# Decoder step: GpSimd's subtractions behind the expert order, sums copied in halves, constant products where TensorE waits, two adaLN products at later attention units

## The chip, the cores and the metric

One core of one Trainium2 chip runs the whole program. The metric is the device time of one execution in microseconds (us); the median of three runs is quoted.

## The reference, cut to what matters

One inference step of a two-layer decoder for 320 tokens (256 of a prompt, 8 sequences of 8 new ones). Layer 0 mixes tokens by sliding-window attention, layer 1 by gated linear attention (GLA); each is followed by a mixture of 64 experts. All weights are fp32 and come from HBM.

```python
for layer in range(DEPTH):
    mod = (jax.nn.silu(c) @ ada_w[layer] + ada_b[layer])[:, None, :]      # adaLN: 12 blocks of 512 columns a layer
    sh1, sc1, g1, sh2, sc2, g2 = jnp.split(mod, 6, axis=-1)
    hmix = rms_norm(x, norm_mix_g[layer]) * (1.0 + sc1) + sh1
    out = attention or gla (hmix)
    x = x + g1 * out
    hffn = rms_norm(x, norm_ffn_g[layer]) * (1.0 + sc2) + sh2
    x = x + g2 * moe(hffn)            # sigmoid router, top 8 of 64 experts, plus one shared expert
return rms_norm(x, final_g), caches, states
```

## The kernel before, in words

Each engine has a program of its own, written out by hand and joined by semaphores; an engine takes its instructions in the order of the code. Weights stream through a ring of five 2 MB slots (`gu_ring`) and one of five 1 MB slots (`dn_ring`), issued in order by SyncE (SP).

- **Front.** The squares, their sum and the mean of x, then four adaLN blocks, one after the other: `ada_part(n)` (L480, eight products of 32 x 512 on TensorE), `ada_copy` (ScalarE, L486), `ada_fold` (L492, four products of 128 x 32), `ada_mod` (VectorE, L499). The next `ada_part` waits for the `ada_mod` before it. Behind them the q, k, v projections (L646) begin.
- **Attention.** A pipeline over 24 units: scores (L691), mask and maximum (VectorE L908, L915), exponential (ScalarE L831), normalisation (VectorE L923), turning of the probabilities (L713), copy (ScalarE L842), output (L727). In unit 2 VectorE also does `rope(2)` (L880 to L883). The table `AT_SLOT` says at which unit i the adaLN blocks 12 to 17 are multiplied; ScalarE copies such a block at the end of its own step i, TensorE folds it in step i + 1.
- **MoE, choice of experts.** TensorE turns h into token rows (L1544); ScalarE writes each twice, as fp32 (`tok32`) and rounded (`hi`); GpSimd subtracts them (`lo`, L1518). VectorE meanwhile picks the top 8 (L1626 to L1652), TensorE counts (L1570) and sorts, VectorE writes `order` (L1667), SP reads it and issues the experts' weights (L1453, L1457). Between these steps TensorE does the shared expert's up products (`shared_up`, L1559, four groups of 16).
- **MoE, passes.** 29 passes (`NP`) of two or four experts: up products (L1822), gathers for the next batch (L1763), turning (L1836), down products (L1853), and `combine` (L1785, L1788), which adds the pass before to the sums in PSUM. After the last pass comes `rest`, a branch that runs only if an expert got more tokens than it has slots; `any_left` loads the number that decides it into a register of each engine.
- **MoE, end.** ScalarE and VectorE copy the sums to SBUF (L1963 to L1970), TensorE turns them back (`back`, L1985), VectorE adds them to x (L402 to L407). After layer 0 come the next norm (L351, L357), two adaLN blocks and GLA (L1038 on); after layer 1 the rows are turned once more (L2046) for the final norm.

## Time and profile before

| what | value |
|---|---|
| runs | 1592.98, 1595.33, 1602.84 us; median 1595.33 |
| profiled execution: its own time, its span | 1602.87 us, 1600.8 us |
| granted TensorE clock, mean | 0.962 of full speed |
| TensorE busy | 1483.1 us (93% of the span) |
| VectorE, ScalarE, GpSimd busy | 413.9, 387.2, 49.3 us |
| DMA | 509.57 MB, mean 318 GB/s |

The span is from the first to the last instruction of the profiled execution; some 2 us lie around it. Busy shares are averages over stages with different limits: what one stage costs has to be read from its own stretch. Times in rows are us from the start of the span. A matmul of two fp32 operands stands as two records in the trace, so eight products are "x16".

### The profile page before, as it was taken

What the parts mean: (1) busy time and instruction counts of PE and PEld (TensorE: products, weight loads), DVE (VectorE), ACT (ScalarE), POOL (GpSimd) and SP (SyncE); (2) the same over time, 40 slices, a digit from 0 to 9 for tenths busy, and PEclk for the clock granted to TensorE, in tenths of its full rate; (3) what the DMA queues carried; (4) which work ended last, traced back from release to release, by engine and by line L of the source; (5) the groups of instructions that cost most, each with busy time, mean ns of one, the idle gap of its engine ahead of it and who ended that gap; (6) DMA issues with size and microseconds to landing.
All of it is one profiled execution on the core that took longest, in us unless ns stands there. A gap on an engine that the chain in (4) does not pass through costs nothing.

```text
span 1600.8 us, 20538 instructions
## 1 busy us (share of the span) xinstructions
PE 1483.1 (93%) x8192; PEld 757.5 (47%) x8192; DVE 413.9 (26%) x978; ACT 387.2 (24%) x1077; POOL 49.3 (3%) x86
## 2 busy tenths in 40 slices
PE   5997998899998899999899989989999999999895
PEld 2444665454453445444345445554444444544433
DVE  2116515121221212211253233432121112211113
ACT  2114404122221112121244212412222211212112
POOL 0000301000000000000100000100000000000000
PEclk9998899999999999999889998999999999999997
DMA  9977514899998999999942243188999999998971
GB/s 396 365 282 290 181 63 164 343 417 421 420 419 322 421 421 418 381 398 421 393 158 105 106 161 115 60 336 342 421 421 420 388 377 421 420 421 343 423 323 33
DMA packets 65888, 509.57 MB, mean 318 GB/s; under 512 B 7776, under 2 KB 8048, under 8 KB 10208
## 3 DMA queue, kind: packets, MB, share of 16 engines
q1 hardware_dynamic: 62064, 490.17, 74.9%
q0 software_dynamic: 3728, 18.07, 3.1%
q8 instruction: 67, 1.10, 0.3%
q14 instruction: 29, 0.24, 0.0%
HBM read 499.16 MB, written 11.01 MB: 319 GB/s over the span
## 4 chain that ended last, share of the span: by engine, by line
PE 80%; DMA 9%; ACT 3%; DVE 3%; issue 2%; SPq 1%; PEld 1%; PEldq 1%; ACTq 0%; DVEq 0%
PE bank L1822 24%; PE banks L1853 11%; DMA s_gu_ring<-in_moe_wu_dram 9%; PE banks L1763 7%; PE banks L426 5%; PE banks L1023 3%; PE ybank L1785 3%; PE banks L1785 3%; PE bank L1788 3%; PE banks L646 3%; PE bank L480 2%; PE banks L1051 2%; PE bank L492 1%; PE bank L1773 1%; PE banks L1028 1%
## 5 line engine op out<-in xcount | busy, mean ns | idle before, releaser
L1822 PE MATMUL bank<-s_gu_ring,s_hbuf 128*32 128x512 f32 (+1 forms) x2560 | 422.9, 613 | 31.6 <-DMA s_gu_ring<-in_moe_wu_dram 31.6
L1822 PEld LDWEIGHTS bank<-s_gu_ring,s_hbuf 128*32 128x32 f32 (+1 forms) x2560 | 134.9, 125 | 310.4 <-issue 310.4
L1853 PE MATMUL banks<-s_dn_ring,s_hTs 128*32 128x512 f32 (+1 forms) x1280 | 211.6, 597 | 2.4 <-ACT s_hTs L1899 2.4
L1951 DVE TENSOR_TENSOR s_ylo<-banks,s_yhi 128x512 fp32r<-128x512 f32 x116 | 80.3, 692 | 338.8 <-ACT s_yhi L1907 338.8
L1763 PE MATMUL banks<-s_sel,s_htok 128*128 128x512 f32 (+2 forms) x640 | 148.6, 381 | 0.5 <-issue 0.5
L1763 PEld LDWEIGHTS banks<-s_sel,s_htok 128*128 128x128 f32 x640 | 110.0, 188 | 61.6 <-issue 45.0
L1907 ACT CAST s_yhi<-banks 128x512 fp32r<-128x512 f32 x116 | 68.0, 586 | 282.0 <-PE banks L1853 282.0
L1946 DVE SCALAR_TENSOR_TENSOR s_hh<-s_sg,s_wsl,bank 128x256 f32<-128x256 f32 x58 | 27.9, 480 | 371.2 <-ACT s_sg L1891 371.2
L1891 ACT ACTIVATE s_sg<-bank 128x256 f32<-128x256 f32 x58 | 22.3, 385 | 410.5 <-PE bank L1822 410.5
L1853 PEld LDWEIGHTS banks<-s_dn_ring,s_hTs 128*32 128x32 f32 (+1 forms) x1280 | 58.8, 122 | 123.7 <-issue 120.9
L1933 DVE COPY s_hbuf<-banks 128x512 f32<-128x512 f32 (+1 forms) x60 | 40.4, 674 | 110.1 <-PE banks L1763 110.1
L1023 PE MATMUL banks<-s_gu_ring,s_hbuf 128*128 128x512 f32 x128 | 55.9, 593 | 0.5 <-DVE s_rs L1307 0.5
L1865 ACT COPY s_hbuf<-banks 128x512 f32<-128x512 f32 (+1 forms) x60 | 34.4, 574 | 80.7 <-PE banks L1763 80.7
L1877 ACT ACTIVATE s_wsl<-s_wall 32x1 f32<-32x1 f32 (+1 forms) x160 | 46.7, 292 | 2.9
L1785 PE MATMUL ybank<-s_yhi,s_gt 128*128 128x512 f32 x116 | 41.4, 439 | 5.3 <-issue 5.3
L480 PE MATMUL bank<-s_gu_ring,s_condT 128*32 128x512 f32 x288 | 38.9, 662 | 5.3 <-DVE s_mod L499 4.7
L646 PE MATMUL banks<-s_gu_ring,s_hbuf 128*128 128x512 f32 x96 | 42.7, 597 | 1.3 <-ACT s_hbuf L389 1.3
L426 PE MATMUL banks<-s_qk,s_gu_ring 128*128 128x320 f32 x128 | 37.2, 454 | 0.8 <-ACT s_qk L1244 0.8
L1023 PEld LDWEIGHTS banks<-s_gu_ring,s_hbuf 128*128 128x128 f32 x128 | 24.2, 191 | 29.1 <-issue 28.2
L426 PE MATMUL banks<-s_hbuf,s_gu_ring 128*128 128x320 f32 x128 | 36.8, 450 | 0.6 <-DVE s_hbuf L932 0.6
L1785 PE MATMUL banks<-s_yhi,s_gt 128*128 128x512 f32 x116 | 36.8, 399 | 0.0
L1788 PE MATMUL bank<-s_yhi,s_gt 128*128 128x512 f32 x116 | 36.5, 395 | 0.0
(414 smaller groups left out, 1518.0 us busy)
## 6 DMA issues: line engine op xcount, KB each, us to landing
s_gu_ring<-in_moe_wg_dram SPq DMA_DIRECT2D x128, 1024.0 KB, 13.5
s_gu_ring<-in_moe_wu_dram SPq DMA_DIRECT2D x128, 1024.0 KB, 15.6
s_dn_ring<-in_moe_wd_dram SPq DMA_DIRECT2D x128, 1024.0 KB, 14.8
s_gu_ring<-in_ada_w_dram SPq DMA_DIRECT2D x24, 2048.0 KB, 11.9
s_gu_ring<-in_win_dram SPq DMA_DIRECT2D x6, 2048.0 KB, 12.3
s_gu_ring<-in_wqkv_dram SPq DMA_DIRECT2D x3, 2048.0 KB, 20.1
s_gu_ring<-in_wo_dram SPq DMA_DIRECT2D x2, 2048.0 KB, 7.9
s_gu_ring<-in_shared_up_dram SPq DMA_DIRECT2D x2, 2048.0 KB, 13.4
```

Source lines behind the costliest of these rows:

```text
L426: last = pe.matmul(b[:, 0:T], item(slot)[:, k, (m % 4) * P:(m % 4 + 1) * P], src[:, k, :], start=(k == 0), stop=(k == KC - 1))
L480: last = pe.matmul(ada_bank(n)[32 * j:32 * j + 32, :], condT[:, k, :], item(s)[:, k, :], start=(kk == 0), stop=(kk == 1))
L646: last = pe.matmul(b[:, :], hT[:, k, t0:t0 + P], item(slots[cch])[:, k, :], start=(k == 0), stop=(k == KC - 1))
L1023: last = pe.matmul(b[:, :], hT[:, k, t0:t0 + P], w[:, k, :], start=(k == 0), stop=(k == KC - 1))
L1763: last = pe.matmul(b[:, width * x:width * x + width], w[:, m * P:(m + 1) * P], sel[:, s, 0:width], start=(n == 0), stop=(n == 4))
L1785: pe.matmul(acc[(t, half)], g[:, t * P:(t + 1) * P], y[:, half, :], start=False, stop=(p == NP - 1 and y is ylo))
L1788: last = pe.matmul(bank[6][:, :], g[:, 320 - 64 * half:448 - 64 * half], y[:, half, :], start=False, stop=(p == NP - 1 and y is ylo and ha ...
L1822: last = pe.matmul(W0[o:o + n, :], tokens_of(p, k)[:, o:o + n], w[:, k, :, :], start=(k == 0), stop=(k == KC - 1))
L1853: last = pe.matmul((W1, W2)[half][o:o + n, :], hTs[:, f, o:o + n], dn_ring[:, dn_of[(l, r)][0], w0:w0 + 512], start=(f == 0), stop=(f == 1))
L1877: act.activation(wsl[p % 2][o:o + n, 0:1], w[:, 0:1], ACT.Identity, bias=w[:, 1:2])
L1907: act.copy(yhi[:, half, :], (W1, W2)[half]).then_inc(S["y_high"], 1)
L1951: dve.tensor_tensor(ylo[:, half, :], (W1, W2)[half], yhi[:, half, :].bitcast(F32), ALU.subtract).then_inc(S["y_low"], 1)
```

## The change

1. **Order first.** GpSimd waits for `order_full` of the layer before its three subtractions.
2. **Constant products.** A new function `keep_awake(pe, b, n)` issues n products of the identity and a block of ones (128 x 128, fp32) into a bank that nobody reads then. It is called after each of the first four `ada_part` (3 products) and `ada_fold` (7, 7, 7, 5), in attention step 3 after the fold (5), after the last pass's down products (10), after the last `combine` (8), and after the two adaLN folds between layer 0 and GLA (10).
3. **adaLN blocks 12 and 13** move from attention steps 0 and 4 to 2 and 5; the other four stay.
4. **Sums in halves.** ScalarE copies the samples' rows first, then the first tile in two halves of 512 columns; VectorE its tile in two halves. `acc_out` comes after the first halves, a new `acc_out2` after the second; `back` waits for that at m = 4.
5. **Register load.** `any_left` moves from behind the last pass to ahead of it, on all three engines; the branch stays where it was.
6. A semaphore of GLA that nobody waited for (`qprod_full`) is gone.

```diff
@@ -406,6 +406,11 @@
+        def keep_awake(pe, b, n):
+
+            for _ in range(n):
+                pe.matmul(b[:, 0:P], ident, ones, start=True, stop=True)
+
...
@@ -544,8 +549,8 @@
                 AT_SLOT = {}
                 AT_SLOT[-1] = 11
-                for n in range(12, 18):
-                    AT_SLOT[4 * (n - 12)] = n
+                for n, i in zip(range(12, 18), (2, 5, 8, 12, 16, 20)):
+                    AT_SLOT[i] = n
...
@@ -609,7 +614,9 @@
                     pe.wait_ge(F["cond"], 1)
                     for n in range(4):
                         ada_part(pe, n)
+                        keep_awake(pe, bank[6], 3)
                         ada_fold(pe, n)
+                        keep_awake(pe, bank[6], 7 if n < 3 else 5)
...
@@ -746,6 +753,8 @@
                             scores(i)
                         if i - 1 in AT_SLOT:
                             ada_fold(pe, AT_SLOT[i - 1])
+                        if i == 3:
+                            keep_awake(pe, bank[6], 5)
                         if 2 <= i < U + 2:
                             probs_turned(i - 2)
                         if i >= 3:
...
-                    "diff_full", "qk_psum", "qk_full", "decay_full", "qprod_full", "ke_exp", "ke_full", "r_psum", "r_full",
+                    "diff_full", "qk_psum", "qk_full", "decay_full", "ke_exp", "ke_full", "r_psum", "r_full",
...
-                    dve.tensor_tensor(qi[:, :, :], eb[:, :, :], qk[:, 0:4, :], ALU.mult).then_inc(G["qprod_full"], 1)
+                    dve.tensor_tensor(qi[:, :, :], eb[:, :, :], qk[:, 0:4, :], ALU.mult)
...
@@ -1509,6 +1518,7 @@
                     def _(pool):
                         normed(pool, 2 * l + 1)
                         pool.dma_start(h_saved, hbuf[:, 0:KC * T]).then_inc(S["h_kept"], 16)
+                        pool.wait_ge(S["order_full"], l + 1)
                         for t, (t0, tn) in enumerate(TILES):
...
@@ -1806,6 +1816,8 @@
                     slot_weights(0).then_inc(S["tr_full"], 1)
 
                     for p in range(NP):
+                        if p == NP - 1:
+                            left = any_left(pe)
...
@@ -1853,9 +1865,11 @@
                                     last = pe.matmul((W1, W2)[half][o:o + n, :], hTs[:, f, o:o + n],
                                                      dn_ring[:, dn_of[(l, r)][0], w0:w0 + 512], start=(f == 0), stop=(f == 1))
                             last.then_inc(S["y_full"], 1)
+                    keep_awake(pe, W0, 10)
                     pe.wait_ge(S["y_low"], 2 * (l + 1) * NP)
-                    rest_pe(pe)
+                    rest_pe(pe, left)
                     combine(NP - 1).then_inc(S["acc_full"], 1)
+                    keep_awake(pe, W0, 8)
...
+                        if p == NP - 1:
+                            left = any_left(act)
...
+                        if p == NP - 1:
+                            left = any_left(dve)
...
                 acct = hbuf[:, 0:3 * D].rearrange("p (t d) -> p t d", d=D)
 
                 @block.scalar
                 def _(act):
                     act.wait_ge(S["acc_full"], l + 1)
-                    act.copy(acct[:, 0, :], ybank[:, :, :].rearrange("p a b -> p (a b)"))
                     act.copy(acct[0:NS, 2, 0:512], bank[6][0:NS, :])
-                    act.copy(acct[0:NS, 2, 512:1024], bank[6][NS:P, :]).then_inc(S["acc_out"], 1)
+                    act.copy(acct[0:NS, 2, 512:1024], bank[6][NS:P, :])
+                    act.copy(acct[:, 0, 0:512], ybank[:, 0, :]).then_inc(S["acc_out"], 1)
+                    act.copy(acct[:, 0, 512:1024], ybank[:, 1, :]).then_inc(S["acc_out2"], 1)
 
                 @block.vector
                 def _(dve):
                     dve.wait_ge(S["acc_full"], l + 1)
-                    dve.tensor_copy(acct[:, 1, :], pair[1][:, :, :].rearrange("p a b -> p (a b)")).then_inc(S["acc_out"], 1)
+                    dve.tensor_copy(acct[:, 1, 0:512], pair[1][:, 0, :]).then_inc(S["acc_out"], 1)
+                    dve.tensor_copy(acct[:, 1, 512:1024], pair[1][:, 1, :]).then_inc(S["acc_out2"], 1)
...
         def back(pe, l, i, acct, b, m, lag):
 
+            if m == KC // 2:
+                pe.wait_ge(S["acc_out2"], 2 * (l + 1))
...
@@ -2005,6 +2027,7 @@
                     ada_part(pe, n)
                 for n in ada_pair(i):
                     ada_fold(pe, n)
+                keep_awake(pe, W0, 10)
...
             def any_left(eng):
-                eng.wait_ge(S["gt_full"], (l + 1) * NP)
+                eng.wait_ge(S["gt_full"], l * NP + 1)
                 return eng.value_load(excess[0:1, 0:1], min_val=0, max_val=T) > 0
 
-            def rest_act(act):
+            def rest_act(act, left):
                 act.wait_ge(S["y_full"], 2 * (l + 1) * NP)
-                with act.If(any_left(act)):
...
-            def rest_pe(pe):
-                with pe.If(any_left(pe)):
+            def rest_pe(pe, left):
+                with pe.If(left):
```

TensorE at the start of attention, from the fold of block 11 on (`s_kT,s_qT` are scores, `s_gu_ring,s_condT` an adaLN block, `s_cst,s_asb` its fold, `s_cst,s_sc` turned probabilities, `s_pT,s_qkv` outputs). Before:

```order
L492 MATMUL bank<-s_cst,s_asb_0 128x32 x4
L480 MATMUL bank<-s_gu_ring,s_condT 32x512 x8
L691 MATMUL banks<-s_kT,s_qT 128x128 x2
L492 MATMUL bank<-s_cst,s_asb_0 128x32 x4
L691 MATMUL banks<-s_kT,s_qT 128x128 x2
L713 MATMUL ybank<-s_cst,s_sc_0 128x128 x2
L691 MATMUL banks<-s_kT,s_qT 128x128 x2
L713 MATMUL ybank<-s_cst,s_sc_0 128x128 x2
L727 MATMUL bank<-s_pT_0,s_qkv 64x128 x2
```

Now (`s_cst` alone is a constant product):

```order
L497 MATMUL bank<-s_cst,s_asb_0 128x32 x4
L698 MATMUL banks<-s_kT,s_qT 128x128 x4
L720 MATMUL ybank<-s_cst,s_sc_0 128x128 x2
L485 MATMUL bank<-s_gu_ring,s_condT 32x512 x8
L698 MATMUL banks<-s_kT,s_qT 128x128 x2
L497 MATMUL bank<-s_cst,s_asb_0 128x32 x4
L412 MATMUL bank<-s_cst 128x128 x5
L720 MATMUL ybank<-s_cst,s_sc_0 128x128 x2
L734 MATMUL bank<-s_pT_0,s_qkv 64x128 x2
```

The block and its fold have gone behind three pairs of scores and one turning, and five products stand between the fold and the second turning.

TensorE around the last pass of a layer. Before:

```order
L1788 MATMUL bank<-s_ylo,s_gt 128x512 x2
L1853 MATMUL banks<-s_dn_ring,s_hTs 64x512 x8
L2120 TENSOR_LOAD s_excess
L2120 ISA x2
L2151 COMPARE_AND_BRANCH
```

Now, from the down products of the pass before the last:

```order
L1865 MATMUL banks<-s_dn_ring,s_hTs 64x512 x8
L2143 TENSOR_LOAD s_excess
L2143 ISA x2
L1834 MATMUL bank<-s_gu_ring,s_hbuf 64x512 x16
L1848 MATMUL bank<-s_cst,s_hh 128x128 x2
...
L1865 MATMUL banks<-s_dn_ring,s_hTs 64x512 x8
L412 MATMUL bank<-s_cst 128x128 x10
L2174 COMPARE_AND_BRANCH
```

The load stands a whole pass earlier, and its place is taken by ten products.

GpSimd, choice of experts of layer 0: the saving of h, then the three subtractions. Before:

```order
L1511 DMA h_saved<-s_hbuf 128x2560 [waits norm_hs_full,norm_h_full]
L1518 ISA
L1518 TENSOR_TENSOR s_htok<-s_tok_0_0,s_htok 128x1024 [waits tok_hi]
L1518 TENSOR_TENSOR s_htok<-s_tok_1_0,s_htok 128x1024 [waits tok_hi]
L1518 TENSOR_TENSOR s_htok_0<-s_hbuf,s_htok_0 64x1024 [waits tok_lo,tok_hi]
```

Now:

```order
L1520 DMA h_saved<-s_hbuf 128x2560 [waits norm_hs_full,norm_h_full]
L1528 ISA
L1528 TENSOR_TENSOR s_htok<-s_tok_0_0,s_htok 128x1024 [waits tok_hi,order_full]
L1528 TENSOR_TENSOR s_htok<-s_tok_1_0,s_htok 128x1024 [waits tok_hi]
L1528 TENSOR_TENSOR s_htok_0<-s_hbuf,s_htok_0 64x1024 [waits tok_lo,tok_hi]
```

The first has a second wait; nothing else moves on GpSimd.

## Rows read from the trace of the kernel before

**Rows 1.** The page, part 4: chain that ended last, by engine.

```profile
PE 80%; DMA 9%; ACT 3%; DVE 3%; issue 2%; SPq 1%; PEld 1%; PEldq 1%; ACTq 0%; DVEq 0%
```

**Rows 2.** Timeline, choice of experts, layer 0: start, us, engine, line, operation, idle before.

```profile
254.48 4.67 POOL L1518 TENSOR_TENSOR s_htok<-s_tok,s_htok 128x1024 fp32r<-128x1024 f32 x2 [3.31 <-ACT s_htok L1615]
254.84 2.06 DVE L1634 TENSOR_TENSOR s_gs<-s_t 128x24 f32<-128x24 f32 x1
...
256.88 4.47 PE L1559 MATMUL banks<-s_hbuf,s_gu_ring 128*128 128x320 f32 x16
256.93 0.30 DVE L1636 MAX8 s_m<-s_gs 128x8 f32<-128x8 f32 x3
...
257.94 1.25 DVE L1642 TENSOR_TENSOR s_gm<-s_gr,s_gs 128x24 f32<-128x24 f32 x1
...
262.38 0.19 PE L1570 MATMUL bank<-s_mb,s_upper_b 128*128 128x64 bf16 x1 [1.03 <-issue]
...
264.98 0.21 DVE L1667 CAST s_order<-bank 1x64 int32<-1x64 f32 x1
...
265.44 0.36 DVE L1670 SCALAR_TENSOR_TENSOR s_pw<-s_pw,s_sm 128x192 f32<-128x192 f32 x1
265.71 0.35 DVE L1672 SCALAR_TENSOR_TENSOR s_pw<-banks,s_mb 128x192 f32<-128x192 f32 x1
...
267.94 0.52 PEld L1589 LDWEIGHTS banks<-s_cst,s_pw 128*128 128x128 f32 x3
```

**Rows 3.** Timeline, just before the first pass of layer 0.

```profile
295.98 0.17 ACT L1878 COPY s_wsl<-s_wall 32x1 f32<-32x1 f32 x1
297.33 8.63 PE L1822 MATMUL bank<-s_gu_ring,s_hbuf 128*32 128x512 f32 x64 [2.96 <-DMA s_gu_ring<-in_moe_wu_dram]
```

**Rows 4.** Timeline, front.

```profile
24.00 3.61 PE L480 MATMUL bank<-s_gu_ring,s_condT 128*32 128x512 f32 x16 [1.22 <-DVE s_mod L499]
...
28.31 1.08 PE L492 MATMUL bank<-s_cst,s_asb 128*128 128x32 f32 x8 [0.70 <-ACT s_asb L486]
...
29.77 1.92 PE L480 MATMUL bank<-s_gu_ring,s_condT 128*32 128x512 f32 x16 [0.38 <-DVE s_mod L499]
...
38.83 7.11 PE L646 MATMUL banks<-s_gu_ring,s_hbuf 128*128 128x512 f32 x16 [1.28 <-ACT s_hbuf L389]
```

**Rows 5.** Timeline, start of attention.

```profile
125.05 3.04 DVE L880 TENSOR_TENSOR s_rot<-s_qkv,s_cst_swa 128x640 f32<-128x640 f32 x4
...
131.06 0.69 PE L713 MATMUL ybank<-s_cst,s_sc 128*128 128x128 f32 x2 [4.95 <-DVE s_sc L923]
...
134.30 3.08 PE L480 MATMUL bank<-s_gu_ring,s_condT 128*32 128x512 f32 x16
```

**Rows 6.** Timeline, end of layer 0's MoE.

```profile
789.20 1.19 PE L1785 MATMUL ybank<-s_yhi,s_gt 128*128 128x512 f32 x2 [2.68 <-issue]
...
793.54 1.01 ACT L1963 COPY s_hbuf<-ybank 128x1024 f32<-128x1024 f32 x1 [6.39 <-PE bank L1788]
...
795.67 0.99 PE L1985 MATMUL bank<-s_cst,s_hbuf 128*128 128x128 f32 x3 [2.17 <-ACT s_hbuf L1965]
```

**Rows 7.** Timeline, start of GLA.

```profile
819.00 2.09 PE L1038 MATMUL bank<-s_hbuf,s_wa 128*32 128x320 f32 x16 [2.79 <-ACT s_hbuf L389]
...
821.61 1.89 PE L1043 MATMUL banks<-s_a1T,s_wa 128*128 128x320 f32 x4 [0.52 <-ACT s_a1T L1166]
```

**Rows 8.** Timeline, end of layer 1's MoE and final stage.

```profile
1571.21 0.70 PE L1785 MATMUL ybank<-s_yhi,s_gt 128*128 128x512 f32 x2 [2.60 <-issue]
...
1574.23 1.01 ACT L1963 COPY s_hbuf<-ybank 128x1024 f32<-128x1024 f32 x1 [4.99 <-PE bank L1788]
...
1581.19 0.48 DVE L402 SCALAR_TENSOR_TENSOR s_xT<-bank,s_mod,s_xT 128x256 f32<-128x256 f32 x1 [0.68 <-PE bank L1985]
```

**Rows 9.** Windows: stretch, us, busy us (instructions) by engine, granted clock, DMA share, GB/s.

```profile
819.40:822.70 3.30, 2.78 (x18) 1.17 (x10) 0.00 (x0) 0.43 (x1) 0.00 (x0) 0.50 1.00 427
1577.20:1590.00 12.80, 11.74 (x45) 7.46 (x43) 6.51 (x24) 3.17 (x11) 0.00 (x0) 0.50 0.00 0
```

More of the change, by code:

```diff
@@ L2134, in rest_act, with rest_dve @@
                         act.wait_ge(sums_in, it + 1)
-            def rest_dve(dve):
-                with dve.If(any_left(dve)):
+            def rest_dve(dve, left):
+                with dve.If(left):
                     with dve.Fori(0, NE) as it:
@@ L2173, in rest_pe @@
                         last.then_inc(sums_in, 1)
-            return rest_pe, rest_act, rest_dve
+            return any_left, rest_pe, rest_act, rest_dve
         qkv_slots, qkv_in, win_slots, win_in = [], [], {}, {}
```

9 lines of the change are left out of this document (5 added, 4 removed).

## The prediction

> **What bounds the kernel now.** First the chain by engine [rows 1]: TensorE carries 80% of it and the DMA 9%. So an edit pays only where TensorE, or a transfer that it waits for, moves. I then read the timeline in seven places that the change touches, each time for the wait that ends last.
>
> In the choice of experts [rows 2] VectorE loses time to GpSimd. A TENSOR_TENSOR of 24 columns takes 2.06 us at 254.84 and ends at 256.90, where GpSimd's first subtraction ends (254.48 plus half of 4.67 is 256.8); the next, of the same size, takes 1.25 us and ends at 259.19, where the second ends. The MAX8 between them, with GpSimd busy, takes 0.30. The counting on TensorE waits for this chain and starts at 262.38, after 1.03 us of idleness; ahead of it stands the first group of the shared expert, which ends at 256.88 + 4.47 = 261.35. The first pass starts when its weights have landed, 297.33, 1.18 us after ScalarE's last preparation, 295.98 + 0.17 = 296.15 [rows 3].
>
> At the front TensorE waits in short steps for ScalarE and VectorE, and one adaLN block takes 3.61 us where the next takes 1.92 [rows 4]. In attention it waits 4.95 us for `rope(2)`, and then does a block in 3.08 us [rows 5]. At the end of a layer's MoE it waits 2.68 and 2.60 us before the last `combine` and 2.17 for the copies [rows 6, 8]. Between layer 0 and GLA it waits 2.79 us, and the granted clock behind that is 0.50 of full speed, 1.2 GHz [rows 7, 9].
>
> **What one constant product takes.** No row shows it. A projection takes 7.11 us for 16 records of 512 columns, 0.44 each; 128 columns take a quarter, and two records 0.22 us. The fold's four products of 32 columns take 1.08 us, 0.27 each, paced by the weight loads [rows 4]. I take 0.22, the nearer in width, and 0.27 as the upper end; at 1.2 GHz twice 0.22, 0.44.
>
> **Order first.** With GpSimd held back, the two waits of VectorE go (2.06 + 1.25 less some 0.3 of work for both), and a third before the top-8 mask: over 3 us. But TensorE is busy with the shared group until 261.35, so the counting moves only from 262.38 to about 261.4: 1.0 us, and `order`, the issue of the weights and the first pass with it. The preparation on TensorE moves by the same 1.0. GpSimd's three operations now run from about 264.3 to 271.5 (4.67 + 2.5 us), long before the preparation that reads them ends (296.15). What they can hold up is `pw`: L1670 has two operands in SBUF and would wait for the first subtraction to end, 266.6, then take 0.36; L1672 has one in PSUM and ends at about 267.3; before it ended at 265.71 + 0.35. TensorE took `pw` at 267.94, now at 266.94, so 0.35 us late: less than the 1.18 us of spare time in rows 3. Gain 1.0 us a layer, 2.0 in all. Ends: 0, if `pw` comes later still, and 3.0 a layer if TensorE's group were not next.
> The Trainium skill (SBUF — State Buffer, Who interferes with whom) says that a VectorE instruction with two SBUF inputs contends with a GpSimd instruction that reads SBUF, and that one with at most one SBUF input, outside the 2-port modes, does not. The trace agrees for the 2.06 and the 0.30 us; no row shows an instruction with one input in PSUM beside GpSimd, and by that rule L1672 runs free, as I took it. It is `pw` on which this hangs: see the first rival.
>
> **Front** [rows 4]. Three products (0.66) fit in the 0.70 that the fold waits for ScalarE. Seven (1.54) do not fit in the 0.38 in front of a block: +1.16 each for blocks 2 and 3. Block 1 waited 1.22 for VectorE's long work and starts 0.4 later. In return TensorE has hardly a gap before it, and I expect 1.92 in place of its 3.61: -1.69. The last five (1.10) fit in 1.28. Sum 0.4 - 1.7 + 1.2 + 1.2 + 0.2 for edges: +1.3 us. Ends: 0 and, with 0.27 each and no faster block, +4.
>
> **Attention** [rows 5]. Block 12 (1.92 and a wait of 0.38, as in rows 4) leaves the way to the second scores, so `rope(2)` starts 2.3 us earlier, at 122.8, and what it held back with it: the second turning could start at 128.8. But ScalarE copies block 12 at the end of its step 2, behind an exponential that waits for `rope(2)` and ends near 129.0; with two copies behind it (some 0.4 and 0.6) that makes 130.0. The fold follows, 1.08 us at full speed and up to 2 at 1.2 GHz, then five products, 1.1 to 1.7 as the clock comes up between. So the turning that stood at 131.06 starts between 132.3 and 133.7: 1.2 to 2.6 late. Behind it I save 1.16 in block 13 (3.08 to 1.92) and some 0.5 in the small products around it, slow before (0.69 for two turnings). Sum between -0.5 and +1.0; I take +0.5, nearer the slow fold since TensorE idles ahead of it, with ends -1 and +2.5.
>
> **Register load.** Of the 2.68 and 2.60 us before the last `combine` [rows 6, 8] the load goes; the copying of the last sums and the branch stay. TensorE's sequencer runs ahead of its queue in the last pass but one, as far as the long rows of weight loads go, so I cost the load at nothing there; with that cover gone it would be under 1 us. In the old place now stand ten products, 2.2 us: that, and no longer the load, is what `combine` waits for. Gain 0.45 a layer, 0.9. Ends -1 (a loss, if load and products add up) and 0.9, since the products bound it.
>
> **Clock under combine.** In layer 0 the sums take 789.20 to 793.54, 4.34 us; in layer 1, at full speed, 1571.21 to 1574.23, 3.02 us [rows 6, 8]. Ten products in front keep TensorE busy through the gap: -1.3.
>
> **Copies in halves.** From the end of `combine` to the first `back` it is 795.67 - 793.54 = 2.13 us. Of this 1.01 is the first tile's 1024 columns on ScalarE [rows 6]; the samples' two copies stay. With 512 columns in its place, and a fixed part in each copy, I take off a third of it: -0.35 a layer, -0.7; ends 0 and -0.5 a layer. VectorE is never last. The eight products (1.76) just fit. The first `back` at full speed (it took 0.99 with three records) gives another 0.3 in layer 0.
>
> **GLA start.** The ten products (2.2) fit in 2.79. L1038 and L1043 ran mostly at 1.2 GHz [rows 7, 9]; at full speed 16 records of 320 columns in groups of 32 take 1.92 x 320/512 = 1.2 in place of 2.09, and L1043 1.3 in place of 1.89: -1.4. Ends 0 and, if the products ran at half speed (4.4 in a gap of 2.79), +1.6.
>
> **Final stage.** VectorE's 24 instructions in 12.8 us are eight steps (`back`, add, turning) of 1.6 or, without the edges, 1.55 us at 1.2 GHz, and VectorE is idle 0.68 in each [rows 8, 9]. The eight products should keep full speed for the first two or three steps, at some 1.05 us, since most of the 0.68 goes: -1.1. Ends 0 and -3.5 (all seven steps). Here TensorE is busy 11.74 of 12.80 us and still at 0.50: turnings alone have not lifted the clock.
> The Trainium skill (TensorE: Matmul & The Clock Gate, Part 4: PE-mode transpose) says that transposes do not count as busy for the clock gate. The trace agrees in that row; by the rule the gain ends after the first steps, as taken. If turnings counted once the clock is up, it would be the -3.5.
>
> **Sum.** -2.0 + 1.3 + 0.5 - 0.9 - 1.3 - 0.7 - 0.3 - 1.4 - 1.1 = -5.9 us. The profiled execution took 1602.87 and would take 1597.0; it was a slow one of its kind, 7.5 over the median. From the median 1595.33 I get **1589.4 us**.
>
> **Rivals.**
> - *GpSimd now holds up `pw`.* If an operand in PSUM doesn't free L1672, it waits for the second subtraction as well, 2.3 us more; the preparation is then 0.35 + 2.3 = 2.65 late, 1.5 more than the spare time, and the 2.0 us are gone with 0.5 a layer on top. For: the 2.06 us; against: only TENSOR_TENSOR from SBUF is seen held. About 1592.
> - *The end stages stay at full speed.* 2.4 less in the final stage and 1 to 2 less in the norm behind layer 0: 1585.5. Against: 0.50 with 92% busy.
> - *Slower: the products run at 1.2 GHz and lift nothing.* Then each takes 0.44, and ten take 4.4 in gaps of 2.7: place, the end of layer 0. Front +4, attention +2, `combine` +1.7, copies +1.4 a layer, GLA +1.6, less the 2.0 of the order: +10, 1605. It decides from about 0.3 us a product. For: TensorE idles 4.95 us before rows 5's slow block, and one row of the front is slow after work; against: the combine of layer 1 ran at full speed after a gap of 2.60.
> - *The change does nothing that counts*: DMA sets the pace of the passes behind (a 1 us earlier start is caught by the waits for weights), and gains and losses of TensorE cancel: 1595.
>
> **Chances.** Forecast 0.58, `pw` 0.12, end stages 0.10, slow products 0.10, nothing 0.10. The runs of before spread over 10 us, so a median of three moves by 3 or so. The range 1581 to 1600 takes in the forecast with its ends, the `pw` case, the end stages and the nothing case, and leaves out most of the slow products. About 1% (16 us) is what a measurement of this kernel can tell from no change: faster by more needs nearly every favourable end at once, 0.04; slower by more needs more than the slow products give, 0.03; within it 0.93.
>
> **What would show it.** Right: L1634's like at 0.2 us and counting 0.1 us behind the shared group; GpSimd beginning behind `order`; L1672's like at 267.3 on this scale; block 1 at 1.92 us and the first projection 1 to 2 us later; the second turning of attention behind the five products; `combine` 2.2 us after the last down product and 3.0 long in both layers; no gap beside the register load before the last pass; L1038's like at 1.2 us; a final stage whose first steps take 1.05 and whose last take 1.55. Wrong: a constant product above 0.3 us, a first pass that doesn't start earlier against the norm ahead of it, or a gap in front of the last pass.

## The result, and the profile after it

| | runs | median, us | range, us | against the kernel before |
|---|---|---|---|---|
| before | 6 | 1594.15 | 1591.27 to 1602.84 | |
| changed | 6 | 1582.22 | 1574.63 to 1583.48 | 0.990 [0.987, 0.993] |
| changed, other series | 5 | 1577.81 | 1574.92 to 1583.31 | 0.9886 [0.9858, 0.9914] |

The last column is the ratio to the kernel before, with its 95% interval. The change takes 12 us off in the first series and some 20 in the second, where 13 runs of the kernel before had a median of 1598.44. The forecast was a gain of 5.9, to 1589.4. The first series lies inside the stated range (1581 to 1600), near its lower end, the second below it, and the gain is at least twice the forecast. The kernel before, measured again as `e17`, gave 0.9975 [0.9951, 0.9998] against itself, an interval that leaves out 1: ratios that differ by 0.0025 (4 us) or less tell little here, and an interval that just misses 1 proves no gain. What a stage is worth is therefore read from profiles, of which there are 20 in all, those of the two kernels counted.

The page of the changed kernel, its clock and its chain (PEclk is the granted clock in tenths, 40 slices of the span; 1.00 is 2.4 GHz, 0.50 is 1.2 GHz):

```profile
PEclk9998989999999999999999998999999999999998
...
PE 80%; DMA 9%; DVE 3%; ACT 3%; issue 1%; SPq 1%; PEldq 1%; PEld 1%; ACTq 0%; DVEq 0%
```

The chain has not moved against [rows 1]. The mean granted clock is 0.978, before it was 0.962.

Choice of experts, layer 0 (answers to [rows 2]):

```profile
260.22 0.20 DVE L1644 TENSOR_TENSOR s_gs<-s_t 128x24 f32<-128x24 f32 x1
...
261.46 0.18 DVE L1652 TENSOR_TENSOR s_gm<-s_gr,s_gs 128x24 f32<-128x24 f32 x1
...
262.27 4.47 PE L1569 MATMUL banks<-s_hbuf,s_gu_ring 128*128 128x320 f32 x16
...
266.57 0.19 PE L1580 MATMUL bank<-s_mb,s_upper_b 128*128 128x64 bf16 x1
...
269.48 4.77 POOL L1528 TENSOR_TENSOR s_htok<-s_tok,s_htok 128x1024 fp32r<-128x1024 f32 x2 [12.92 <-DVE s_order L1677]
269.64 2.40 DVE L1680 SCALAR_TENSOR_TENSOR s_pw<-s_pw,s_sm 128x192 f32<-128x192 f32 x1
271.96 0.34 DVE L1682 SCALAR_TENSOR_TENSOR s_pw<-banks,s_mb 128x192 f32<-128x192 f32 x1
```

VectorE's two waits are gone (0.20 and 0.18 for 2.06 and 1.25), and the counting begins without a gap behind the shared group. GpSimd now runs behind the order. The first operation of `pw`, with both operands in SBUF, takes 2.40 and ends at 272.04, 0.2 behind GpSimd's first subtraction (269.48 plus half of 4.77); the second, with one operand in PSUM, takes 0.34 beside GpSimd's second.

The front (answers to [rows 4]; L412 is a constant product):

```profile
23.87 1.92 PE L485 MATMUL bank<-s_gu_ring,s_condT 128*32 128x512 f32 x16 [0.22 <-DVE s_mod L504]
25.73 0.94 PE L412 MATMUL bank<-s_cst 128*128 128x128 f32 x6
26.50 1.07 PE L497 MATMUL bank<-s_cst,s_asb 128*128 128x32 f32 x8
27.41 1.81 PE L412 MATMUL bank<-s_cst 128*128 128x128 f32 x14
29.14 1.92 PE L485 MATMUL bank<-s_gu_ring,s_condT 128*32 128x512 f32 x16
...
39.41 1.10 PE L653 MATMUL banks<-s_gu_ring,s_hbuf 128*128 128x512 f32 x2
```

Seven products take 1.73 us from start to start, 0.25 each with the edges. The first projection starts 0.6 us later than before, and no block behind the first is slow. (The first took 2.75 us here, 3.40 in the kernel before and 1.92 in its second profile, `e17`. The record of the clock begins only at 19.2 us here and at 20.6 in the kernel before, and a window counts nothing as lost ahead of it.)

Attention (answers to [rows 5]):

```profile
123.72 1.92 PE L485 MATMUL bank<-s_gu_ring,s_condT 128*32 128x512 f32 x16
125.57 0.49 PE L698 MATMUL banks<-s_kT,s_qT 64*128 64x128 f32 x4
130.33 1.92 PE L497 MATMUL bank<-s_cst,s_asb 128*128 128x32 f32 x8 [4.26 <-ACT s_asb L491]
132.06 2.48 PE L412 MATMUL bank<-s_cst 128*128 128x128 f32 x10
134.33 0.64 PE L720 MATMUL ybank<-s_cst,s_sc 128*128 128x128 f32 x2
...
138.10 1.99 PE L673 MATMUL ybank<-s_cst,s_qkv 128*128 128x128 f32 x10 [1.46 <-issue]
...
142.00 3.63 PE L485 MATMUL bank<-s_gu_ring,s_condT 128*32 128x512 f32 x16
```

TensorE waits 4.26 us for block 12's copy, which stands on ScalarE behind the exponential. Fold and products hold up the second turning to 134.33; then there is a new gap of 1.46, and block 13 takes 3.63 us. In the kernel before, block 13 stood just there (134.30 to 137.38 in [rows 5]) and the turnings at L673, then L666, followed without a gap:

```profile
137.31 1.09 PE L666 MATMUL ybank<-s_cst,s_qkv 128*128 128x128 f32 x8
```

End of layer 0 (answers to [rows 6] and [rows 7]) and final stage (answers to [rows 8]):

```profile
786.52 2.50 PE L412 MATMUL bank<-s_cst 128*128 128x128 f32 x20
...
788.77 0.71 PE L1795 MATMUL ybank<-s_yhi,s_gt 128*128 128x512 f32 x2
...
791.61 1.95 PE L412 MATMUL bank<-s_cst 128*128 128x128 f32 x16
791.81 0.58 ACT L1981 COPY s_hbuf<-bank 64x512 f32<-64x512 f32 x1 [4.59 <-PE bank L1798]
...
792.99 0.59 ACT L1983 COPY s_hbuf<-ybank 128x512 f32<-128x512 f32 x1
...
793.63 0.64 PE L2007 MATMUL bank<-s_cst,s_hbuf 128*128 128x128 f32 x3
...
812.90 1.28 PE L1047 MATMUL bank<-s_hbuf,s_wa 128*32 128x320 f32 x16 [0.48 <-issue]
...
1565.09 0.48 DVE L402 SCALAR_TENSOR_TENSOR s_xT<-bank,s_mod,s_xT 128x256 f32<-128x256 f32 x1 [0.16 <-PE bank L2007]
```

Windows of the same profile (columns as in [rows 9]): from the first `back` to L1052, and from the first `back` of layer 1 to the last turning.

```profile
793.63:814.72 21.09, 19.24 (x127) 9.54 (x127) 13.58 (x39) 11.96 (x24) 5.30 (x11) 0.92 0.75 298
1560.50:1569.50 9.00, 7.91 (x48) 5.21 (x48) 6.62 (x24) 3.85 (x10) 0.00 (x0) 1.00 0.00 0
```

This is the surprise. The same turnings that ran at 0.50 for 12.8 us in [rows 9] run at 1.00 to the last of them, eight steps in 9.0 us. Behind layer 0 the clock still fell in this profile, for 3.4 us (0.92 over the window).

### The profile page after: what moved, and what is told of

Read it like the earlier page. It is cut to its first block, busy times and chain, and to the rows that moved or that the text cites. A ratio compares the mean times of both kernels' runs of the same rounds, so it can differ in the third digit from the quotient of the medians.

```text
span 1581.0 us, 20900 instructions
## 1 busy us (share of the span) xinstructions
PE 1484.3 (94%) x8370; PEld 773.3 (49%) x8370; DVE 409.8 (26%) x980; ACT 387.3 (24%) x1079; POOL 49.2 (3%) x86
## 4 chain that ended last, share of the span: by engine, by line
PE 80%; DMA 9%; DVE 3%; ACT 3%; issue 1%; SPq 1%; PEldq 1%; PEld 1%; ACTq 0%; DVEq 0%
PE bank L1834 24%; PE banks L1865 11%; DMA s_gu_ring<-in_moe_wu_dram 9%; PE banks L1773 7%; PE banks L431 5%; PE banks L1032 3%; PE ybank L1795 3%; PE banks L1795 3%; PE bank L1798 3%; PE banks L653 3%; PE bank L485 2%; PE banks L1060 2%; PE bank L497 1%; PE bank L412 1%; PE bank L1783 1%
## 5 line engine op out<-in xcount | busy, mean ns | idle before, releaser
L1834 PE MATMUL bank<-s_gu_ring,s_hbuf 128*32 128x512 f32 (+1 forms) x2560 | 415.6, 602 | 28.3 <-DMA s_gu_ring<-in_moe_wu_dram 28.3
L1032 PEld LDWEIGHTS banks<-s_gu_ring,s_hbuf 128*128 128x128 f32 x128 | 24.2, 191 | 29.1 <-issue 28.2
```

Of the source, the lines that this page charges most:

```text
L1032: last = pe.matmul(b[:, :], hT[:, k, t0:t0 + P], w[:, k, :], start=(k == 0), stop=(k == KC - 1))
L1834: last = pe.matmul(W0[o:o + n, :], tokens_of(p, k)[:, o:o + n], w[:, k, :, :], start=(k == 0), stop=(k == KC - 1))
```

## The experiments

### One edit at a time on the kernel before

`e1_order_only` adds `pool.wait_ge(S["order_full"], l + 1)`. `e2_end_products_only` adds the products at the layers' ends:

```diff
+                    keep_awake(pe, W0, 10)
                     pe.wait_ge(S["y_low"], 2 * (l + 1) * NP)
                     rest_pe(pe)
                     combine(NP - 1).then_inc(S["acc_full"], 1)
+                    keep_awake(pe, W0, 8)
...
                 for n in ada_pair(i):
                     ada_fold(pe, n)
+                keep_awake(pe, W0, 10)
```

> The kernel before, and only GpSimd's wait for the expert order added. The order ends 1.0 to 1.2 us earlier against the norm in each layer. Theory A (what starts earlier ends earlier): the time falls by 2.0 to 2.4 us, to 1592. Theory B (the weight transfers pace the passes, and take in what is won or lost ahead of them): the first pass of a layer starts 1.2 us earlier and the passes behind it give it back at their waits for weights; 1594, no change. In both no gain above 1%.

Measured: 1591.63, 0.9961 [0.9935, 0.9986]. The choice of experts (first turning of h to counting) goes from 10.73 to 9.54 us, and in layer 1 from 10.71 to 9.53. The first pass starts with it (44.34 and 44.15 us behind the first turning of h, against 45.67 and 45.52 before), and the passes behind it are no longer than in the first profile. The stage speaks for theory A; the time, 2 us beside `e17`'s ratio, cannot tell 1592 from 1594.

> The kernel before, and only the products at the end of a layer's MoE (10 and 8) and ahead of GLA (10). Theory A (most of the 12 us comes from the clock at these ends): combine of layer 0 in 3.0 us, the final stage's eight steps at 0.9 to 1.0 us, no granted clock of 0.50 behind the last combine but in one stretch; against the kernel before 4 us less in the final stage, 4 to 6 behind layer 0, 1.3 in combine: 1594 falls to 1584 to 1586. Theory B (the 12 us are mostly fewer clock drops at the waits of the passes, by chance): these stages give at most 4, 1590.

Measured: 1588.16, 0.9937 [0.9912, 0.9962], 10 us, or 6 beside `e17`'s ratio. From the first `back` to the second small product of GLA (L1052 in the changed kernel, L1043 before) takes 20.15 us, and the first `back` of layer 1 to VectorE's last instruction 16.17 (before 25.94 and 20.18). The stages are theory A's; the time lies between the two. The old copies leave a gap of 0.39 us ahead of `back` here, and the clock held at 1.00 all the same.

### The changed kernel with one edit taken back

`e3_no_end_products` is the changed kernel without the 10, 8 and 10 products; `e4_attention_as_before` has

```diff
-                for n, i in zip(range(12, 18), (2, 5, 8, 12, 16, 20)):
-                    AT_SLOT[i] = n
+                for n in range(12, 18):
+                    AT_SLOT[4 * (n - 12)] = n
...
-                        if i == 3:
-                            keep_awake(pe, bank[6], 5)
```

> The changed kernel without the products at the end of a layer's MoE (10 and 8) and ahead of GLA (10); everything else as changed. Theory A: the clock is at 0.50 again behind the last combine of both layers, the final steps take 1.5 to 1.6 us each, and the time goes from 1582 to 1591 to 1593. Theory B: 1585.

Measured: 1589.10, 0.9948 [0.9925, 0.9972]. Window, final stage:

```profile
1562.50:1575.00 12.50, 12.26 (x46) 7.92 (x47) 6.72 (x24) 3.80 (x9) 0.00 (x0) 0.51 0.01 1
```

TensorE is busy 98% of it and stays at half clock; the same work, begun at full clock and without a gap ahead of it, keeps it. Here the gap ahead of `back` was 1.86 us, and the clock fell 0.1 us after its start:

```profile
1562.55 1.55 PE L2005 MATMUL bank<-s_cst,s_hbuf 128*128 128x128 f32 x5 [1.86 <-ACT s_hbuf L1981]
```

That is theory A in the profile, and by the ratio too (8 to 10 us over the changed kernel).

> The changed kernel with the adaLN blocks 12 to 17 at their old units and without the five products in attention. The profile of the changed kernel has attention end 4.8 us later against its start than before. Theory A (that loss reaches the end): 1577, 4 to 5 under the changed kernel. Theory B (the passes of layer 0 wait for weights, 4 us at two places, and take it in): 1582, no difference, with the wait for weights longer by what the start is earlier. The forecast had this edit at -0.5.

Measured: 1574.88, 0.9848 [0.9816, 0.988]. From the first scores to the last output of the prompt (start to start, as for attention in all that follows) 75.92 us, in the changed kernel's first profile 82.72. The time is theory A's and more: by the ratio 6 to 8 us under the changed kernel. In the repeats below (`e0` 79.07, `e9` 79.08 us) the difference in attention is gone, and the one in time is smaller. Why the transfers did not take the loss in is argued, not shown: the choice and the issue of the weights come later with attention.

`e0_changed_again` repeats the changed kernel; `e5_no_front_no_attention` is `e4` without the front's products, `e7_units_without_products` drops only the five in attention.

> The changed kernel once more, as the yardstick of this chip and for a second profile. Theory A (its gain is one of stages): ratio to the kernel before 0.990 to 0.992, combine 3.0 us in both layers, the eight final steps at 0.93 us each, attention 4 to 5 us longer from its first scores to its last output than in the kernel before. Theory B (the profile had luck): a ratio of 0.995, with final steps at 1.55.

Measured: 1577.81, 0.9886. Theory A at the layers' ends (final stage 16.17 us, 1.00), but not in attention: 79.07 us, only 1.2 more than the first profile of the kernel before, where 4 to 5 were expected. Block 13 took 1.92 us here.

> The changed kernel without the products at the front and in attention and with the adaLN blocks at their old units; the order, the copies, the load and the products at the layers' ends as changed. Theory A (both earlier edits cost their own time, 1.2 us at the front and 5 to 7 in attention): ratio to the kernel before 0.984, some 8 us under the changed kernel, the first projection at 38.3. Theory B (the front's products keep the clock and pay for themselves in the first blocks of attention too): 0.986 or more, and slower than the version with the front's products.

Measured: 1583.67, 0.9919 [0.9892, 0.9946], slower than `e4` and than the changed kernel. That is theory B by its words, though it gave no reason for 7 us. The first projection started at 44.18 and attention at 126.68, 7 us late.

> The changed kernel without the five products in attention; the adaLN blocks stay at their new units. Theory A (the loss in attention comes from block 12's copy behind the exponential, and from what is late behind it): attention is still 2.5 to 4 us longer than before, and the time 1 to 2 us under the changed kernel. Theory B (the five products themselves make the loss): 4 to 6 us under it.

Measured: 1577.88, 0.9871 [0.9841, 0.9901], the same as `e0` in the same series. Theory B (4 to 6 us) falls by the time, and theory A's 1 to 2 us are not seen either. The profile does not isolate the five products: the second turning comes 12.5 us behind the first scores, with them 14.8, but two later blocks took 3.52 and 3.58 us, and attention as a whole 82.31.

### The front

`e8_front_only` is the kernel before with the front's products, `e10_front_as_before` the changed kernel without them, `e14_three_at_the_front` is `e4` with the threes and without the sevens and the five.

> The kernel before, and only the products at the front added. In three of the profiles without them the clock drops there for 3.4 us and block 1 takes 3.3 to 3.6 us; in one it stays down from 21.6 to 48.9, the first projection starts at 44.2 and attention 7 us later than with them. Theory A (without the products the long drop is common, with them it does not occur): the first projection at 38.4 to 39.6 in the profile, and the time 3 to 7 us under the kernel before. Theory B (the long drop is rare, and the products cost the forecast's 1.3 us): the same as the kernel before or 1 us above.

Measured: 1595.56, 0.997 [0.9948, 0.9992], no different from `e17`'s 0.9975, so the time does not decide. The profile has theory A's front: the clock at 1.00 and the first projection at 38.84.

> The changed kernel without the products at the front only. Theory A: ratio 0.992 to 0.994, 5 us or more over the changed kernel, with runs spread over more than 8 us since the long drop comes in some of them. Theory B (the products cost 1.3): ratio 0.988.

Measured: 1585.13, 0.9896 [0.9862, 0.993], runs from 1575.93 to 1589.87. The spread is theory A's, the ratio between the two.

> The changed kernel with attention as it was, and at the front only the three products ahead of each fold, none behind it. With all front products this kernel measured 0.985 and 0.987 of the kernel before, without any 0.992. Theory A (the three fill the gap at no cost and hold the clock): 0.984 to 0.986, the first projection at 37.5 to 38.5. Theory B (the gaps behind VectorE's work, up to 2.7 us, decide, and only the seven cover them): a drop at the front in the profile, 0.989 to 0.992.

Measured: 1578.28, 0.9862 [0.9829, 0.9896]. By the ratio A, by the profile B (0.90 below). Not settled by the time.

Windows of the first 50 us, in this order: the kernel before as first shown, before again (`e17`), `e5`, `e14`, `e8`.

```profile
0.00:50.00 50.00, 32.33 (x152) 12.60 (x153) 8.04 (x17) 14.70 (x30) 3.07 (x9) 0.97 0.97 402
```

```profile
0.00:50.00 50.00, 30.38 (x127) 12.81 (x128) 8.04 (x17) 13.53 (x28) 3.07 (x9) 0.80 0.95 392
```

```profile
0.00:50.00 50.00, 30.30 (x122) 13.03 (x123) 8.04 (x17) 13.53 (x28) 3.07 (x9) 0.73 0.96 393
```

```profile
0.00:50.00 50.00, 33.66 (x172) 15.96 (x173) 8.04 (x17) 14.67 (x30) 3.08 (x9) 0.90 0.97 403
```

```profile
0.00:50.00 50.00, 37.33 (x228) 20.60 (x229) 8.04 (x17) 14.70 (x30) 3.07 (x9) 1.00 0.97 404
```

The granted clock is the third number from the end. Seven profiles have the front of before (the two of the kernel before, `e1`, `e2`, `e5`, `e10`, `e15`): three have 0.97, the others 0.83, 0.80, 0.73 and 0.73. All twelve with all the front's products have 1.00. The timeline of the kernel before, second profile:

```profile
17.19 1.92 PE L480 MATMUL bank<-s_gu_ring,s_condT 128*32 128x512 f32 x16
...
23.60 3.64 PE L480 MATMUL bank<-s_gu_ring,s_condT 128*32 128x512 f32 x16 [2.70 <-DVE s_mod L499]
27.94 1.92 PE L492 MATMUL bank<-s_cst,s_asb 128*128 128x32 f32 x8 [0.69 <-ACT s_asb L486]
30.23 3.64 PE L480 MATMUL bank<-s_gu_ring,s_condT 128*32 128x512 f32 x16 [0.38 <-DVE s_mod L499]
...
36.87 3.18 PE L480 MATMUL bank<-s_gu_ring,s_condT 128*32 128x512 f32 x16 [0.38 <-DVE s_mod L499]
...
43.12 3.53 PE L646 MATMUL banks<-s_gu_ring,s_hbuf 128*128 128x512 f32 x4 [1.28 <-ACT s_hbuf L389]
```

Here block 0 ran at full clock and ended early, so the wait for VectorE behind it was 2.70 us, where [rows 4] have 1.22. Behind it the clock stayed at half for three blocks, and the projection started 4.3 us later than in the first profile. In all four profiles whose block 0 took 1.92 us and whose front lacked the sevens (`e5`, `e14`, `e15`, `e17`) the wait behind it was 2.70 or 2.71 us, and block 1 took 3.64. In `e14`, where the threes close the next gap, block 2 was back at 1.92; in the other three it took 3.64 as well.

### What holds the clock at the layers' ends

`e6_turnings_for_products` replaces the ten and eight products by

```diff
+                pe.transpose(b[:, 0:P], ones, ident)
```

`e12_turnings_for_the_same_time` has 19 and 15 of these; `e13_eight_without_ten` drops the ten products.

> The changed kernel, and the ten and eight products at the end of a layer's MoE replaced by as many turnings (transposes of the 128 x 128 block of ones into the same bank); those at the front, in attention and ahead of GLA stay. Theory A (what keeps the clock is that TensorE has no gap, whatever it does): the same time as the changed kernel, final steps at 0.93 us. Theory B (turnings do not count, products do): the clock falls behind the last combine as without them, final steps at 1.55 us for all or most of the stage, 4 to 7 us slower than the changed kernel.

Measured: 1584.19, 0.9921 [0.9898, 0.9945]. Ten turnings took 1.31 us, ten products 2.50, so a gap of 0.99 us stayed ahead of `back`:

```profile
1557.03 1.21 PE L2012 MATMUL bank<-s_cst,s_hbuf 128*128 128x128 f32 x6 [0.99 <-ACT s_hbuf L1988]
```

The clock fell for part of the final stage (0.81 from 1557 to 1566) and rose again with nothing but turnings running:

```profile
1559.10:1562.30 3.20, 3.20 (x14) 2.22 (x13) 1.81 (x8) 0.00 (x0) 0.00 (x0) 0.50 0.00 0
1562.60:1569.10 6.50, 4.13 (x26) 2.68 (x25) 3.36 (x12) 3.66 (x12) 0.00 (x0) 1.00 0.00 0
```

In layer 0, with the same gap of 0.99 us, it did not fall. The run cannot decide between its theories, since ten turnings do not fill what ten products fill: the time, 6 us over `e0`, is theory B's, but the stage in the profile lost only 1.3 of it.

> The changed kernel with 19 and 15 turnings in place of the ten and eight products at the end of a layer's MoE. A turning of this size took 0.13 us in the run with ten and eight of them, a product 0.25, so these fill the same 2.5 and 1.9 us and leave no gap. Theory A (gaps decide, not the kind of work): 0.988 to 0.990 of the kernel before, as with products, the eight final steps at 0.93. Theory B (turnings do not count): 0.992 or more as with ten and eight, with a drop in the final stage.

Measured: 1579.00, 0.9866 [0.9834, 0.9898]. Final stage:

```profile
1559.00:1568.00 9.00, 7.81 (x50) 5.21 (x48) 6.63 (x24) 4.09 (x10) 0.00 (x0) 1.00 0.00 0
```

Theory A: turnings that fill the gap (0.23 us of it was left ahead of `back`) do what products do.

> The changed kernel without the ten products ahead of the last combine; the eight behind it and the ten ahead of GLA stay. Theory A (the last gap before the stage decides): combine starts 0.2 us earlier, the clock in the final stage holds and the time stays within 2 us of the changed kernel, 0.989. Theory B (both gaps are needed, since the clock answers late to the first): drops in combine or in the final steps, 0.992 to 0.994.

Measured: 1578.76, 0.9869 [0.9842, 0.9896]; the final stage 16.17 us, as with the ten. In layer 0 `combine` fell to half clock:

```profile
781.45 0.70 PE L1795 MATMUL ybank<-s_yhi,s_gt 128*128 128x512 f32 x2 [1.94 <-DVE s_ylo L1968]
...
783.62 1.06 PE L1795 MATMUL ybank<-s_ylo,s_gt 128*128 128x512 f32 x2
```

In layer 1, after a gap of 1.91, it did not. By the time and the final stage that is theory A; the drop in `combine` is theory B's. The gap ahead of `back` decides for the stage; the ten are worth one `combine` now and then. No run separates the ten products ahead of GLA from the eight.

### A better version, and what was left in the passes

`e9` repeats `e4`; `e11_products_in_the_long_wait` is `e4` with `keep_awake(pe, bank[6], 17)` ahead of the second turning.

> The changed kernel with attention as it was (blocks 12 to 17 at their old units, no five products), again, beside a kernel without the products at the front. If the first ratio of 0.985 was of the kernel: 0.984 to 0.987 and some 4 us under the changed kernel. If it was of the sample: 0.988 or more.

Measured: 1579.67, 0.9865 [0.9835, 0.9895], within what was expected if the first ratio was of the kernel; the gain over the changed kernel is smaller than in the first sample, and attention was 79.08 us, no less than `e0`'s.

> The changed kernel with attention as it was, and 17 products (4.3 us at 0.25 each) in the 4.95 us that TensorE waits there ahead of the second turning. Theory A (the clock follows the gap): no drop at 126 to 137, block 13 in 1.92 us in place of 2.4 to 3.1, the turnings and outputs around it in 0.44 in place of 0.7; 2 to 3 us under the same kernel without them. Theory B (the drop comes later instead, or the products delay the turning): no difference or 1 us slower.

Measured: 1576.69, 0.9849 [0.9818, 0.9879] (1576.45 without one of the six executions, which took 3829.43 us for a reason that nothing on record shows). Timeline:

```profile
127.20 4.06 PE L412 MATMUL bank<-s_cst 128*128 128x128 f32 x34
132.22 0.44 PE L720 MATMUL ybank<-s_cst,s_sc 128*128 128x128 f32 x2 [0.96 <-DVE s_sc L932]
...
134.55 1.92 PE L485 MATMUL bank<-s_gu_ring,s_condT 128*32 128x512 f32 x16
```

Locally theory A: no drop around block 13, which takes 1.92. Against `e4` and `e9` (75.92 and 79.08 us) attention takes 75.85; the time is 3 us under `e9`, 2 over `e4`, and cannot tell them apart.

> The kernel before, and only the copies in halves, the earlier register load and the dropped semaphore. By the stages that they touch they are worth 0.3 us of copies and 0.7 of load in each layer. Theory A (no more than that): 2 us under the kernel before, 0.9985. Theory B (the load in its old place also slows the 29 passes: the four profiles with it have 462.3 and 463.2 us from the first pass to the 28th, the thirteen others 459.0 and 460.1): 459 to 460 us in both layers, 8 us under, 0.995.

Measured: 1596.06, 0.9964 [0.9938, 0.9991]; from the first pass to a mark near its 28th, 460.35 and 460.74 us in the two layers. Beside `e17`'s 0.9975 that is 2 us, theory A's; the interval by itself holds both theories, and the passes lie between the two, nearer to theory B's.

> The kernel before with GpSimd's wait for the order, the products at the front and those at the layers' ends; attention, copies and the register load as before. Theory A (copies and load are worth 2 us): 2 us over the version that has them too (0.985 and 0.987), so 0.987 to 0.988. Theory B (the passes are 3 us a layer longer with the load in its old place): 0.990 or more, passes at 462 to 463.

Measured: 1577.13, 0.9854 [0.9814, 0.9893], passes 458.47 and 457.20. Theory B falls: the passes are short without the earlier load too. Theory A's 2 us for copies and load are not seen either: the time is no longer than with them.

> The kernel before once more, for a second profile of it and as the yardstick of the two others. Theory A (the first profile was a slow one by chance in the front, the passes and behind layer 0): ratio 1.000; the choice of experts at 10.7 us, the last combine's gap at 2.6 to 2.7, the final steps at 1.55, as in the first; behind layer 0 23 to 26 us to the second small product of GLA. Theory B: the passes again at 462 to 464 us in both layers, which would speak for the load.

Measured: 1598.22, 0.9975; passes 462.85 and 460.05. The final stage, the gap ahead of the last `combine` and the choice of experts are as in the first profile. The front is not, and against theory A it is slower than in the first profile. Theory B's 462 to 464 us came in one layer of two.

## Why the prediction was wrong

Three terms failed. The final stage was given 1.1 us because turnings were taken to let the clock fall, and gave 4.1; the norm behind layer 0 was given nothing, and gave some 2; and the front was a cost of 1.3 and is a gain of 3.1 on average. The time of the first series still fell inside the range, which says little for the sum: the first profile had the mild case in the front and, in layer 0, a slow `combine` that only some of the other profiles have.

Means over the profiles that have an edit and those that have not, each stage from the start of one row to the start of another (the final one to the end of VectorE's last instruction), beside the terms of the forecast. Front leaves out `e14`, attention `e7` and `e11`, and the two ends of layers `e6`, `e12` and `e13`, since their edits differ. The groups differ in other edits too, so a row is a comparison of groups and no pure effect.

| stage | without, us | with, us | difference | forecast |
|---|---|---|---|---|
| choice of experts, each layer | 10.72 | 9.53 | -1.2 (twice) | -1.0 (twice) |
| front, to the first scores | 122.5 (7 profiles) | 119.4 (12) | -3.1 | +1.3 |
| attention | 77.3 (11) | 79.9 (7) | +2.6 | +0.5 |
| fourth product pair of the last `combine` to `back`, where the clock is full | 3.70 | 3.39 | -0.3 (twice) | -0.35 (twice) |
| last down products to `combine`, layer 1 (before, changed) | 6.26 | 5.84 | -0.4 (a layer) | -0.45 (a layer) |
| `back` of layer 0 to L1052 | 24.2 (6) | 20.4 (11) | -3.8 | -1.7 |
| GLA from there to the next turning of h | 211.9 (6) | 210.2 (14) | -1.6 | 0 |
| final stage | 20.3 (6) | 16.2 (11) | -4.1 | -1.1 |

**Order first.** Right in mechanism and size. `pw` was held up as forecast by the first subtraction (2.40 us) and not by the second, so the first rival did not occur; against the order its weight load starts 0.2 us later (3.18 us behind it, before 2.96), within the spare time.

**Register load, copies, clock under `combine`.** Right: 0.4 for 0.45, 0.3 for 0.35, and in layer 0 the sums take 3.04 us (788.77 to the first copy at 791.81) for 4.34 in [rows 6]. The price of a product was right too: ten take 2.25 us to the start of `combine` (786.52 to 788.77), for 2.2. `e3`, without products, has a gap of 1.94 in place of 2.60 to 2.68, so the load alone frees 0.7 and the ten products take 0.3 of it back. That the slow `combine` stood in layer 0 was the draw of one profile: in the six profiles without products the clock fell under it at six of twelve layer ends, with them at none but `e13`'s one. From its start to the first `back` that is 1.5 us a run on average, a saving that no row of the table holds.

**Final stage: the step that failed most.** "Turnings alone have not lifted the clock ... by the rule the gain ends after the first steps, as taken." The row was right and the conclusion was not: that turnings did not raise a clock that was down does not show that they let fall one that is up. The stage kept 1.00 in every profile with products just ahead of it, -4.1 for -1.1, and `e12` kept it with turnings only. In `e6` the clock even came back from 0.50 during turnings, which it did not do in the kernel before, so the row is no rule for the raising either. The rule of the Trainium skill (TensorE: Matmul & The Clock Gate, Part 4: PE-mode transpose), that transposes do not count as busy in the way that products do, is not borne out by this stage: as the forecast read it, it would have ended the gain after the first steps. The rival "end stages stay at full speed" named what happened; it had a chance of 0.10 and a price of -3.5, which was near.

**Behind layer 0.** The forecast counted the first `back` and GLA's two products (-1.7) and took nothing for the norm between them. From `back` to L1052 it is 20.1 to 20.2 us in nine of the eleven profiles with the products, 21.1 and 21.7 in the two where the clock still fell (the changed kernel's first and `e11`), and 22.5 to 25.9 without.

**Front: wrong in sign.** "I expect 1.92 in place of its 3.61: -1.69" held. But the one profile shown had the mild case, one slow block. In four of seven profiles with this front the clock stayed at half for 17 to 27 us (0.83 to 0.73 over 50 us: the missing share, over 0.5, of 50). The cost was about right: in the three mild profiles the first scores start at 118.6 on average, with the products at 119.4, +0.8. What they prevent was not in the profile. The whole-kernel ratios agree in sign (`e8` beside `e17`, `e10` beside `e0`, `e5` beside `e4`), but for sizes from 1 to 11 us, of which the first two, 1 and 2, are less than can be told from nothing, so -3 is the profiles' value and no more.

**Attention.** Up to the second turning the mechanism was right: the turning was forecast between 132.3 and 133.7, and stands at 134.33 with a front 0.6 later. What the sum left out is what waits around it. TensorE waits 1.3, 4.26 and 1.46 us in all seven profiles with the new units and the five products, 7.0 in place of 4.95; the last of these opens where block 13 stood before. "Behind it I save 1.16 in block 13" held in five of the seven (1.92 or 1.93 us); in the other two, the changed kernel's first and `e10`, the clock fell a second time and the block took 3.63 and 3.64. +2.6 for +0.5, just over the stated end; in the changed kernel's first profile it was 4.8. The two groups overlap (75.9 to 79.1 us, and 78.8 to 82.7).

**The base.** "It was a slow one of its kind, 7.5 over the median" shifted the sum to the median of three runs, 1595.33. Later series of 11 to 28 runs had medians of 1598 to 1601 for the same kernel; part of the 20 us in those series is this.

**Open.** The table sums to -14, and `combine` adds 1.5. The passes add some 3 us a layer: 462.1 and 462.3 on average in the six profiles of the kernel before and of single edits to it (`e1`, `e2`, `e8`, `e15`), 459.0 and 459.7 in the fourteen others. Some 2 us of each 3 are clock (0.986 in the six, 0.991 in the others). Where it falls in the first pass, that costs 1.7:

```profile
301.86 8.77 PE L1822 MATMUL bank<-s_gu_ring,s_hbuf 128*32 128x512 f32 x64 [2.89 <-DMA s_gu_ring<-in_moe_wu_dram]
```

```profile
293.65 7.07 PE L1830 MATMUL bank<-s_gu_ring,s_hbuf 128*32 128x512 f32 x64 [2.18 <-DMA s_gu_ring<-in_moe_wu_dram]
```

The first row is the kernel before (`e17`), the second `e16`. The first pass took 8.6 to 8.8 us at all twelve layer starts of the six profiles, and at five of 28 of the others; the waits ahead of it, 2.0 to 3.0 us, do not separate the two. The changed kernel itself had 8.77 us after a wait of 2.87 and, in `e0`, 7.07 after 2.78. `e16` shows that it is neither the load nor the copies; what it is, is not settled.

**The better version.** Attention as before with the rest of the change gave 0.9848 and 0.9865, with the long wait filled 0.9849, and without copies and load 0.9854; the changed kernel 0.9886 and 0.990. By these ratios each beats the kernel before by 21 to 24 us and the changed one by 3 to 8, the latter with intervals that overlap. That it is better is not shown: `e12` and `e13`, which have the changed attention, gave 0.9866 and 0.9869.

## What to carry to other kernels

Where TensorE has gaps, price a filler by the clock of everything behind it up to the next gap, not by the gap. One profile shows one draw of where the clock falls: read the stage in several executions before a filler is called useless there, and take a stage's value from profiles when runs scatter by more than the effect. That an activity did not raise a clock says nothing on whether it holds one.

## What the hardware did that I had not expected

- The same turnings ran 12.5 us at 0.51 (`e3`) with TensorE busy 98% of the time, and 9.0 us at 1.00 busy 88% (the changed kernel); the difference was whether a gap of 1.9 to 2.2 us stood ahead of them. With 0.39 us or less ahead of `back` the clock held through the final stage in every profile.
- With a gap of 0.99 us ahead (`e6`), the clock fell during the turnings of layer 1 and came back during turnings; in layer 0 it did not fall.
- After a wait of 2.70 us at the front, half clock lasted through three blocks of 3.64 us with gaps of only 0.38 and 0.69 between (`e5`, `e15`); after 1.22 to 1.49 us one block was slow (the kernel before, `e1`, `e2`), after 1.65 two (`e10`).
- VectorE's operation with one operand in PSUM took 0.34 us while GpSimd subtracted; the one with two operands in SBUF took 2.40 for 0.36. The Trainium skill (SBUF — State Buffer, Who interferes with whom) says so, and the trace now agrees on both.
